# A conv-GeGLU decoder layer: the up-projection with the high and low parts of the activations in one 512-column operand, and three of four weight sums by adding DMAs

## What is computed

```python
def conv_glu_ffn(h, w_up, conv_w, conv_b, w_down):
    u = h @ w_up
    c = lax.conv_general_dilated(u, conv_w[:, None, :], window_strides=(1,), padding=[(2, 0)], ...,
                                 feature_group_count=2 * D_FF) + conv_b      # D_FF = 5632
    gate, val = jnp.split(c, 2, axis=-1)
    return (jax.nn.gelu(gate, approximate=True) * val) @ w_down

h = rms_norm(x, g_ffn_pre[l])
f = conv_glu_ffn(h, w_up[l], conv_w[l], conv_b[l], w_down[l])
x = x + rms_norm(f, g_ffn_post[l])
```

## Time and profile before

| | us |
|---|---|
| median of 3 runs | 2048.89 (2047.55 to 2049.93) |
| profiled execution, its own time | 2046.55 |
| its span, first to last instruction | 2044.8 |
| up-projection, chunks 0 and 1 | 105.4 |
| up-projection, chunks 2 to 21 | 806.4 |
| down-projection and end | 445.4 |
| TensorE / VectorE / ScalarE busy | 2002.3 / 1506.7 / 1018.4 |

### The profile page before, as it was taken

The page is one execution under the profiler, slowest core; times in us unless marked ns, Lnnn a source line. Parts: engine busy times, 40 slices in busy tenths (PEclk is TensorE's granted clock), DMA queues, the critical chain, the costliest instruction groups (busy, mean ns, idle before and its releaser), DMA issues.

```text
span 2044.8 us, 31852 instructions
## 1 busy us (share of the span) xinstructions
PE 2002.3 (98%) x12526; PEld 1802.7 (88%) x12526; DVE 1506.7 (74%) x1934; ACT 1018.4 (50%) x1563; POOL 0.7 (0%) x6
## 2 busy tenths in 40 slices
PE   8999999999999889999999999999999999999997
PEld 6888888888887789999999999999999887888785
DVE  5522543444446789888989888988898998889888
ACT  7422433445435655555555555555555654555453
POOL 0000000000000000000000000000000000000000
PEclk9999999999999989999999999999999999999999
DMA  8433232221535623523442343235223896877684
GB/s 320 136 127 119 78 93 83 80 65 63 226 124 190 222 83 129 174 101 111 156 137 101 122 167 115 101 130 173 101 102 115 308 319 234 279 259 228 201 297 158
DMA packets 220306, 323.28 MB, mean 158 GB/s; under 512 B 10543, under 2 KB 142031, under 8 KB 217853
## 3 DMA queue, kind: packets, MB, share of 16 engines
q1 hardware_dynamic: 219484, 316.00, 45.7%
q10 hardware_dynamic: 672, 5.24, 0.6%
HBM read 281.06 MB, written 44.07 MB: 159 GB/s over the span
## 4 chain that ended last, share of the span: by engine, by line
PE 87%; DVE 7%; ACT 3%; issue 2%; DMA 1%; DVEq 0%; SPq 0%; ACTq 0%
PE ring L2099 12%; PE ring L2101 12%; PE ring L2100 11%; PE ring L2360 10%; PE ring L2361 9%; PE ring L2362 9%; PE side L2360 4%; PE side L2361 4%; PE side L2362 4%; PE side L2099 2%; PE side L2100 2%; PE side L2101 2%; PE side L2175 1%; PE side L2148 1%; DVE w_lo L1780 1%
## 5 line engine op out<-in xcount | busy, mean ns | idle before, releaser
L1780 DVE TENSOR_TENSOR w_lo<-q,w_hi 128x1024 fp32r<-128x1024 f32 (+1 forms) x262 | 308.0, 1176 | 88.2 <-ACT w_hi L1271 69.7
L1501 DVE TENSOR_TENSOR w_lo<-raw,w_hi 128x512 fp32r<-128x512 f32 x256 | 169.6, 688 | 275.1 <-ACT w_hi L1054 275.1
L2360 PE MATMUL ring<-s_hi,w_hi 128*128 128x256 f32 x1008 | 287.4, 285 | 7.6 <-ACT snaps L1363 4.3
L2361 PE MATMUL ring<-s_lo,w_hi 128*128 128x256 f32 x1008 | 286.9, 285 | 0.0
L2362 PE MATMUL ring<-s_hi,w_lo 128*128 128x256 f32 x1008 | 286.8, 285 | 0.0
L1780 DVE TENSOR_TENSOR w_lo<-raw,w_hi 128x1024 fp32r<-128x1024 f32 x214 | 249.1, 1171 | 45.0 <-ACT w_hi L1271 26.9
L1054 ACT ACTIVATE w_hi<-raw 128x512 fp32r<-128x512 f32 x256 | 151.6, 623 | 188.2 <-PE ring L2101 172.8
L1271 ACT ACTIVATE w_hi<-q 128x1024 fp32r<-128x1024 f32 x174 | 183.5, 1056 | 97.7 <-PE side L2362 54.2
L2360 PEld LDWEIGHTS ring<-s_hi,w_hi 128*128 128x128 f32 x1008 | 195.2, 194 | 8.1 <-ACT snaps L1363 4.7
L2360 PE MATMUL ring<-a_hi,w_hi 128*128 128x256 f32 x688 | 196.0, 285 | 3.2 <-issue 3.2
L2099 PE MATMUL ring<-w_hi,act_hi 128*128 128x512 f32 x488 | 192.9, 395 | 3.3 <-DVE w_lo L1501 2.7
(11 more groups left out here) (313 smaller groups left out, 4598.9 us busy)
## 6 DMA issues: line engine op xcount, KB each, us to landing
q<-in_w_up SPq DMA_DIRECT2D x65, 1024.0 KB, 4.9
raw<-in_w_in SPq DMA_DIRECT2D x28, 1024.0 KB, 5.4
raw<-in_w_out SPq DMA_DIRECT2D x24, 1024.0 KB, 5.0
raw<-in_w_up SPq DMA_DIRECT2D x23, 1024.0 KB, 6.3
q<-in_w_down SPq DMA_DIRECT2D x66, 256.0 KB, 4.1
raw<-in_w_down SPq DMA_DIRECT2D x66, 256.0 KB, 4.1
q<-in_w_down SPq DMA_DIRECT2D x22, 512.0 KB, 4.1
q<-sa_d SPq DMA_DIRECT2D x22, 512.0 KB, 5.7
```

Source lines behind the costliest of these rows:

```text
L1501: dve.tensor_tensor(w_lo[:, s, q], raw[:, s, q], w_hi[:, s, q].bitcast(F32), ALU.subtract).then_inc(lo_done, 1)
L1780: dve.tensor_tensor(lo, src, hi.bitcast(F32), ALU.subtract).then_inc(hp_lo_done, 1)
L2360: pe.matmul(dst, hi, b_hi, start=first, stop=False, skip_group_check=True)
L2361: pe.matmul(dst, hi, b_lo, start=False, stop=False, skip_group_check=True)
```

## The change

Both parts of an activation operand lie in one tensor (`both`), and a block is two matmuls in place of three: the weights' high part against high and low of the activations side by side (2 x 256 columns), and the weights' low part against the high one (256). So a bank holds two halves, whose sum is the product, and the halves are added ("folded") by VectorE behind the combinations, which work on 512 columns. For chunks 2 to 21 the sums T1, T3 and T4 are made by DMAs that add their source to what stands at the destination, issued by POOL; T2 stays on VectorE. [...] The core of the diff:

```diff
-            def three_more(dst, hi, lo, b_hi, b_lo, first, last):
-
-                pe.matmul(dst, hi, b_hi, start=first, stop=False, skip_group_check=True)
-                pe.matmul(dst, hi, b_lo, start=False, stop=False, skip_group_check=True)
-                return pe.matmul(dst, lo, b_hi, start=False, stop=last, skip_group_check=True)
+            def two(bank, hi_lo, b_hi, b_lo, first, last):
+
+                pe.matmul(bank.rearrange("p (h n) -> p h n", h=2), b_hi, hi_lo, start=first, stop=False,
+                          skip_group_check=True)
+                return pe.matmul(bank[:, 0:HALF_S], b_lo, hi_lo[:, 0, :], start=False, stop=last, skip_group_check=True)
...
-                    mm = three_more(bank, hp_hi[:, h % 4, w], hp_lo[:, h % 4, w], op_hi[:, k, :],
-                                    op_lo[:, k, :], k == 0 and p not in (P6, P5, P3, P4), k == QK - 1)
+                    mm = two(bank, both[LEFT_OF[p]][:, :, k, :], hp_hi[:, h % 4, w], hp_lo[:, h % 4, w],
+                             k == 0 and p not in (P6, P5, P3, P4), k == QK - 1)
...
+            for c in range(2, CHUNKS):
+                pool.wait_ge(hp_lo_done, place(c, P1, 1) + 1)
+                pool.wait_ge(*b_landed("12", c))
+                pool.dma_start(b11_at(c)[:, :, :].rearrange("p k n -> p (k n)"),
+                               b12_at[:, :, :].rearrange("p k n -> p (k n)"), accum_op=ALU.add).then_inc(t1_in, 16)
+                pool.wait_ge(*b_landed("22", c))
+                pool.wait_ge(t1_in, 16 * (c - 1))
+                pool.dma_start(b12_at[:, :, :].rearrange("p k n -> p (k n)"),
+                               raw[:, 0, :], accum_op=ALU.add).then_inc(t3_in, 16)
+                pool.wait_ge(hp_lo_done, place(c, P6, 1) + 1)
+                pool.wait_ge(*b_landed("21", c))
+                pool.dma_start(raw[:, 1, :], b21_at(c)[:, :, :].rearrange("p k n -> p (k n)"),
+                               accum_op=ALU.add).then_inc(t4_in, 16)
...
+            def fold(dst, x, done):
+                dve.tensor_tensor(dst, *halves(x), ALU.add).then_inc(done, 1)
+
             def c11(c, f):
+
+                dve.wait_ge(snap_done, snap_count(c, 0, f))
+                dve.tensor_tensor(kept_p[f], y_bank(f), kept_p[f], ALU.subtract).then_inc(c11_done, 1)
+                dve.wait_ge(c11_done, 2 * c + f + 1)
...
+                fold(c11_first[f] if c < 2 else u_gate[:, f, 0:HALF_S], kept_p[f], c11_folded)
...
+            def c12(c, f):
+                dve.wait_ge(snap_done, snap_count(c, 3, f))
+                u = u_val[:, f, 0:HALF_S]
+                dve.tensor_tensor(u, x_bank(c, f)[:, 0:HALF_S], u, ALU.add).then_inc(c12_done, 1)
...
+                if 1 < c < CHUNKS and s == 0:
+                    make_t(c, "T2")
...
-                    if s == 5:
+                    if s == 5 and c < 2:
                         make_t(c, "T4")
-                    if s == 10 and c > 0:
+                    if s == 5 and c > 0:
                         c11(c, 0)
                         c11(c, 1)
+                    if s in (11, 12):
+                        c12(c, s - 11)
...
-                    if 1 < c < CHUNKS - 1 and s in (11, 12, 13):
-                        make_t(c + 1, ("T1", "T2", "T3")[s - 11])
-                    if c == 1 and s in (12, 13):
-                        make_t(c + 1, ("T1", "T2")[s - 12])
-                    if c == 2 and s == 0:
-                        make_t(c, "T3")
```

More of the change, by code:

```diff
@@ L506, in build @@
         mk_tok = probs_t
-        lefts = ((a11_hi, a11_lo), (a12_hi, a12_lo), (s2_hi, s2_lo), (s1_hi, s1_lo), (s3_hi, s3_lo),
-                 (s4_hi, s4_lo), (a22_hi, a22_lo))
+        both = (a11_both, a12_both, s2_both, s1_both, s3_both, s4_both, a22_both)
+        lefts = tuple((x[:, 0, :, :], x[:, 1, :, :]) for x in both)
+        kept_p = [snaps[:, f, :, :].rearrange("p h n -> p (h n)") for f in range(2)]
+        kept_u2 = (snaps[:, 2, :, :].rearrange("p h n -> p (h n)"), junk32[:, 0:S])
+        c11_first = [junk32[:, S + f * HALF_S:S + (f + 1) * HALF_S] for f in range(2)]
         raw_q = [raw[:, i, :].rearrange("p (k n) -> p k n", n=2 * P) for i in range(2)]
@@ L1350, in snap @@
             def snap(c, i, f):
-                if i < 3:
-                    if c > 0:
-                        used = (c11_kept if c == 1 else c11_done, c21_done, c22_done)[i]
-                        act.wait_ge(used, 2 * (c - 1) + f + 1)
-                    dst = snaps[:, i, f, :]
-                else:
+                if i == 0 and c > 0:
+                    act.wait_ge(c22_folded, 2 * (c - 1) + f + 1)
+                if i == 1 and c > 0:
+                    act.wait_ge(c21_folded, 2 * (c - 1) + f + 1)
+                if i == 1 and c == 0:
+                    act.wait_ge(squared, SQ_M + len(SQUARES))
+                if i == 2:
+                    act.wait_ge(c11_folded, 2 * c + f + 1)
+                if i == 3:
                     if c > 0:
@@ L1398, in after @@
                         snap(c, SNAP_OF.index(p), f)
-                    if c == 0 and p == P7:
+                    if c == 0 and p == P3:
                         snap(1, 0, f)
@@ L1420, in after @@
                     act.wait_ge(left_lo, LEFT_COUNT[-1])
-                    for f in range(2):
-                        act.wait_ge(c11_done, f + 1)
-                        act.activation(u_gate[:, f, 0:HALF_S], snaps[:, 0, f, :], ACT.Copy).then_inc(c11_kept, 1)
+                    keep_c11(0)
+                if c == 1 and s == 8:
+                    act.wait_ge(tapped, 2)
+                    keep_c11(1)
                 i = conv_at(w, c, s)
@@ L1779, in hp_to_lo @@
                     src = half_source(h - H_DOWN)
-                dve.tensor_tensor(lo, src, hi.bitcast(F32), ALU.subtract).then_inc(hp_lo_done, 1)
+                if h < H_DOWN and SEQ[h][1] == P1:
+                    dve.scalar_tensor_tensor(out=lo, in0=src, scalar=-1.0, in1=hi.bitcast(F32), op0=ALU.mult,
+                                             op1=ALU.subtract).then_inc(hp_lo_done, 1)
+                else:
+                    dve.tensor_tensor(lo, src, hi.bitcast(F32), ALU.subtract).then_inc(hp_lo_done, 1)
             def item_to_lo(i):
@@ L1828, in sum_s1 @@
                 add(batch_of(by_token_tile(s1_val[:, :, :]), batch), batch_of(a21, batch), batch_of(a22, batch),
-                    ALU.add)
+                    ALU.subtract)
             def sum_s2(batch):
@@ L1900, in c21 @@
             def c21(c, f):
-                dve.tensor_tensor(u_gate[:, f, HALF_S:S], v_bank(f), snaps[:, 1, f, :],
-                                  ALU.add).then_inc(c21_done, 1)
+                dve.wait_ge(snap_done, snap_count(c, 1, f))
+                dve.tensor_tensor(kept_u2[f], v_bank(f), kept_u2[f], ALU.subtract).then_inc(c21_done, 1)
+                dve.wait_ge(c21_done, 2 * c + f + 1)
+                if c > 0:
+                    dve.wait_ge(tapped, 4 * (c - 1) + 1 + f)
+                fold(u_gate[:, f, HALF_S:S], kept_u2[f], c21_folded)
```

110 lines of the change are left out of this document (62 added, 48 removed).

## The result

The changed kernel takes **2052.99 us** (median of 20 runs, 2048.39 to 2057.59), the kernel before in the same comparison 2047.55 (20 runs, 2045.94 to 2049.93). The ratio is **1.0023 with a 95% interval of 1.0017 to 1.0029**. Forecast were 2020 us and a chance of 0.75 for faster; the time does lie in the range of 2010 to 2062. The profiled execution took 2051.46 us, span 2049.5, 4.7 more than the span of before.

What follows compares the result with a forecast made beforehand. TensorE's pure matmul stream in the up-projection was taken as the bound. 2046.55 - 29.8 + 1 = 2017.8 us; with the shown median 2.3 above the profiled run, 2020, range 2010 to 2062.

Steps and rivals of the forecast that it cites:

- VectorE's share: In steady up-projection chunks, VectorE's busy time would fall from 35.8 to 34.2 us of a 38.8 us chunk.
- So at this clock a matmul costs its columns plus 13.3 ns, whatever its width: Up-projection blocks would fall from 0.360 to 0.3467 us by dropping one fixed cost, saving 29.8 us over 20 chunks.
- The rival with the fixed cost per block: The 13.3 ns belong to a block, not a matmul, so the saving fails: 2044 to 2050 us; chance 0.04.
- VectorE or the strided operand binds: Late low parts on VectorE, or reading two runs, take half the saving: 2034 us; chance 0.07.
- The sign named for being wrong, a wide step over 0.230: In TensorE's timeline, a wide matmul step over 0.230 us instead of 0.227 would show the forecast wrong.
- The adding DMAs are what decides: In chunks 2 to 21, TensorE stalls only if T1's DMA takes over 9.2 us; each us beyond costs 20.
- L: Duration of an adding DMA from issue to landing, taken as 7.7 us, with bounds of 4.9 and 10.5.
- The copies that free a bank are followed by at least one whole product: ScalarE's wider copies, +1.2 us a chunk, stay hidden, as a product of 2.77 us passes before the bank is wanted.
- The path that I did name, T1 to P6's low part: From T1's landing, T2, high part and low part take 4.7 us; P6 starts 11.1 us into the chunk.
- The case of an issue held behind a running VectorE instruction: POOL's DMA issue waits up to 2.29 us: 16 us given back, 2035; middle of a rival with chance 0.10.
- The bounds are -3 and +6; I take +1: Chunks 0 and 1 keep four sums on VectorE and gain folds, 9.9 us more work, taken as +1 us.
- an adding DMA that lands late: Rival in chunks 2 to 21: T1 lands too late and the kernel is slower, 2125 us at 14 us; chance 0.21.

Runs made afterwards that it cites:

- e1b_three: Changed kernel with the wide matmul split into two of 256 columns, start flag on the first only, all else kept; 2066.27 us.
- g3: f2_t1v with three matmuls of 256 columns a block in place of a wide and a narrow one; 2053.57 us.
- e2_one_run: Changed kernel with high and low parts of each 128-row block side by side in SBUF, so the 512 moving columns are one run; time stayed.
- e5_gelu: Changed kernel with the gelu of the chunk before moved two products later; 2046.84 us.
- e3_t1_vector: Changed kernel with T1 and T2 made by VectorE at their old places in the chunk before, T3 and T4 still by adding DMAs; 2047.40 us.
- f3_abba: e5_gelu with the narrow matmul ahead of the wide one in every second block; 2046.66 us.
- e6_t4: Changed kernel with T4 of chunks 0 and 1 made by adding DMAs too; 3.6 us gained.
- f1_all: Changed kernel with the three mends of e5_gelu, e6_t4 and e7_tail together; 9.3 us under the changed kernel.
- g1: f2_t1v with the narrow matmul ahead of the wide one in every second block; 2031.65 us, 0.8% under the kernel before.
- e7_tail: Changed kernel with the last combinations of chunk 21 ahead of the down-projection's low parts on VectorE; 2.7 us gained.
- f4_grouped: e5_gelu with each product's eight wide matmuls first, then its eight narrow ones; 2047.72 us.
- f2_t1v: f1_all with T1 on VectorE at its old place; six executions took 2042.07, 2040.22, 2027.83, 2027.31, 2029.26 and 2027.92 us.
- e1_three: Changed kernel with three 256-column matmuls a block, start flag on both halves of the bank; 6 to 8 us above the 2060 expected.

## Why the prediction was wrong

**What bounds the kernel, and VectorE's share: right.** TensorE's stream set the time, and VectorE has 643.8 us in chunks 3 to 21, 33.9 a chunk against 34.2 forecast.

**"So at this clock a matmul costs its columns plus 13.3 ns, whatever its width": this failed, for 10.7 us.** The remainder was equal at both widths in streams of one width. A stream of wide and narrow in turn was in no row, and I took it as the sum of the two. It has a pace of 0.3467 (my sum) and one of 0.3533, and is mostly at the second; other orders give 0.3483. The mechanism of the gain is real (e1b_three, g3), its size is half of what I took. The rival with the fixed cost per block (2044 to 2050) does not hold either, since 0.3533 is under 0.360. "VectorE or the strided operand binds" had the size (half the saving goes) but not the cause: e2_one_run has no stride and the same paces. The sign named for being wrong, a wide step over 0.230, did come: 0.233 to 0.241 from wide to narrow at the slow pace. The Trainium skill, "TensorE: Matmul & The Clock Gate", section Back-to-back issue gap, gives N/2.4 + 2.5 ns for the gap of isolated matmuls, with the warning that in a stream of weight loads and matmuls both set the spacing; by the formula the saving would be 5.6 us. The trace does not agree: the matmuls of 256 alone stay at 13.3 ns over their columns in e1b_three, and the wide one is worth 12 to 26 us.

**"The adding DMAs are what decides": right that they hold the risk, wrong in where it ends.** L was taken as 7.7 and measured 7.0; the Trainium skill's estimate of 6.8 from "DMA: Bandwidth & Descriptors", section Anatomy of one DMA, and "Collectives: The Full Stack", section on the bandwidth ceiling, agrees. The step that failed is "The copies that free a bank are followed by at least one whole product": true when the copy is on time, but ScalarE's work is in a fixed order, and the copy of P6 (1136.34 in chunk 10) stands behind a gelu (1135.80) that waits for taps, which wait for low parts, which wait for T2. That path was late in half of the chunks at L = 6.8 to 7.5. It costs 4.7 us in chunks 3 to 21. With the gelu moved these waits are gone (e5_gelu), with T1 on VectorE too (e3_t1_vector), and either brings some 6 us over the whole kernel, though only 0.3 and 1.2 of them in these chunks.

The path that I did name, T1 to P6's low part, was worked out rightly but for one term. Its limit was L = 11.1 + 2.8 - 4.7, and the 2.8 is how long before the chunk the DMA is issued. That lead is 2.3 to 2.4 in the steady chunks of the changed kernel, so the limit is some 8.7 there, and the largest L was 7.5. In chunk 2 the DMA goes out 0.7 us after the chunk has begun: the limit is 5.7, so L = 7.4 makes a wait of 1.7, and 1.8 was measured. In f3_abba the lead is 0.6 and the limit 7.0, so L = 8.6 makes 1.6, and 1.7 was measured. The case of an issue held behind a running VectorE instruction did not come up: POOL issues T3 at 1125.30 in its usual 0.86 us while VectorE is in T2 from 1124.83 on.

**Chunks 0 and 1, "The bounds are -3 and +6; I take +1": mis-sized.** They cost 7.05 us, and chunk 2 is another 4.5 over its forecast. VectorE was 9.9 of 10 us busy there before, so added work had little to hide behind; taking T4 away gave back 3.0 us of chunks 0 and 1 (e6_t4), all three mends 4.3 (f1_all). Chunk 2 is two waits, for P6's low part and for P6's copy. The low part is late because VectorE comes out of chunk 1 late: with T1 as a DMA that issue is late (1.8 us), with T1 on VectorE the wait is 2.4 (e3_t1_vector) and 2.6 (g1). The later gelu takes the copy's wait away (e5_gelu). The remaining 3 us of chunks 0 and 1 stay open.

**The down-projection's start was not in the prediction: 7.7 us, some 6 of them at its start.** TensorE wants a bank that the last combination of chunk 21 has still to read, and on VectorE low parts, the longer combinations and their folds now stand ahead of it. With it moved ahead the wait fell to 1.1 us (e7_tail). After the stall came the lower clock, as in the earlier trace rows; but after the same wait in e2_one_run it did not come, so what the clock cost (some 3 us here, 1.8 near the end) is seen and not explained.

The misses sum to 33.5 us, a little more than the gain that was forecast. That the time lies in the stated range is luck: the range was made wide for an adding DMA that lands late, and none of the misses is that. Small slips in the prediction's sums changed nothing: 12 x 0.7 + 4 x 0.34 is 9.8 and not 9.9, and L = 11.4 would be 2064, not 2062.

Open is why wide and narrow in turn have two paces. The stride is excluded as a cause (e2_one_run); stalls and the first adding DMA are not needed for the slow one (e3_t1_vector). The order of the two is shown to matter (f3_abba, f4_grouped, g1_t1v_abba), by what mechanism is not.

## What to carry to other kernels

A step time is only known for the sequence in which it was measured: before a gain of some ns a matmul is multiplied by thousands, the new sequence itself needs a measurement, and another order of the same instructions may be the better one. When a sum or a load moves nearer to its use, follow every in-order queue behind it to its end, the copies that free banks above all; the first thing that is late was here not what reads the data. When a stall has been mended, look at the whole stage and not at the waits alone: here the stages behind the mends were nearly as long as before, because the faster pace went with the stalls. And a change in a steady loop should be priced at the loop's two ends as well, where there is no slack: here they took 18 of 33 us, 1.8 of which are not shown to belong to the change.

## What the runs showed of the hardware that was not expected

- Matmuls of 512 and 256 columns in turn ran at 0.3467 or 0.3533 us a pair, steadily, with the switch only at a stall; wide, narrow, narrow, wide ran at 0.3483, eight and eight at 0.349. Without a stall from chunk 3 on, the profiled executions of e3_t1_vector and f2_t1v kept 0.3533 for all 266 products.
- Two matmuls that both carried the start flag, into the two halves of one bank, did not leave the whole sum (e1_three); with the flag on the first alone they did (e1b_three). The two kernels differ in nothing else.
- An adding DMA of 1 MB from SBUF to SBUF landed after 7.0 us, with POOL busy 0.86 us for the issue; single ones took up to 8.7 us in f3_abba and 9.1 in e5_gelu.
- A wait of 3.3 us was followed by 14 matmuls at the lower clock (0.43 us for 512 columns); the same wait in e2_one_run was followed by none, and so was one of 1.1 us in e7_tail. Near the end a wait of 1.96 us was followed by the lower clock in the changed kernel, one of 1.95 was not in the kernel before.
